# Two hybrid transformer blocks on one core: banks begun at their first product, four steps of side work later, filler products gone

## The reference, cut to what matters

```
first block, a layer:
  h = rms_norm(x) @ w_in          # queries, keys, values, index heads, gates: 10,052 columns
  y_a = attention over the 64 tokens that an indexer picks (top_k)  @ w_oa
  y_b = silu(layer_norm(conv31(glu)))  @ w_ob
  y_c = (gb * conv3(gc * xc))          @ w_oc
  y_d = stick-breaking attention       @ w_od
  x = x + (sum of sigmoid(gate_i) * y_i) @ w_merge
  x = x + (silu(conv3(h2 @ w_gate)) * (h2 @ w_up)) @ w_down
second block, a layer:
  c_q, c_kv, ... = split(rmsnorm(x) @ w_in_2)
  y_mla  = causal attention on up-projected latents (mla_mixer)
  y_gdn  = gated delta rule: gc = cumsum(g); decay = exp(gc_i - gc_j); triangular solve
  y_moba = block attention with a bias table
  x = x + concat(y_mla, y_gdn, y_moba) @ w_out
```

## Time and profile before

| | us |
|---|---|
| median of three runs | 1325.55 |
| lowest and highest run | 1325.3, 1328.61 |
| the profiled execution | 1327.21 |
| its span | 1325.4 |
| PE busy in it | 1301.4 (98%) |
| DVE, ACT busy | 1026.0 (77%), 746.5 (56%) |
| granted clock of PE, mean | 0.997 |

### The profile page before, as it was taken

How to read it: one execution, slowest core, us unless ns; L and a number is a source line. 1 busy time by engine, 2 the same in 40 slices (tenths; PEclk the granted TensorE clock), 3 DMA queues, 4 the chain that set the end, 5 groups by cost and what they waited for, 6 DMA issues and landing times. The chain is left out here.

```text
span 1325.4 us, 26400 instructions
## 1 busy us (share of the span) xinstructions
PE 1301.4 (98%) x10796; PEld 1240.3 (94%) x10796; DVE 1026.0 (77%) x1763; ACT 746.5 (56%) x1149; POOL 47.3 (4%) x48
## 2 busy tenths in 40 slices
PE   9999999999999999999999999999999999999997
PEld 8899999999999999999999989999989899888996
DVE  6899998677777677999997768777778746677565
ACT  6544566556454465544757556544567445586364
POOL 0000000000000000100000000000001100001100
PEclk9999999999999999999999999999999999999999
DMA  8565455565555465646365555665654223343232
GB/s 279 190 201 181 160 161 189 163 220 186 196 191 191 153 229 176 215 162 197 126 210 167 197 184 178 207 203 193 206 163 152 64 97 128 122 143 112 81 101 75
DMA packets 108991, 223.62 MB, mean 169 GB/s; under 512 B 6180, under 2 KB 17700, under 8 KB 108872
## 3 DMA queue, kind: packets, MB, share of 16 engines
q1 hardware_dynamic: 106736, 218.99, 49.5%
q10 hardware_dynamic: 2136, 2.96, 0.7%
HBM read 220.88 MB, written 1.06 MB: 167 GB/s over the span
## 5 line engine op out<-in xcount | busy, mean ns | idle before, releaser
L1191 ACT ACTIVATE whi<-ring 128x1024 fp32r<-128x1024 f32 (+3 forms) x430 | 433.7, 1027 | 343.2 <-PE bank L513 221.3
L1764 DVE TENSOR_TENSOR wlo<-ring,whi 128x1024 fp32r<-128x1024 f32 (+3 forms) x430 | 496.9, 1180 | 166.0 <-ACT whi L1191 133.1
L513 PE MATMUL bank<-hhi,whi 128*128 128x256 f32 x2016 | 272.5, 277 | 2.5 <-ACT hhi L1228 1.8
L522 PE MATMUL bank<-hhi,wlo 128*128 128x256 f32 x2016 | 273.0, 277 | 1.0 <-DVE wlo L1764 1.0
L513 PE MATMUL bank<-hlo,whi 128*128 128x256 f32 x2016 | 269.1, 276 | 0.0
L513 PEld LDWEIGHTS bank<-hhi,whi 128*128 128x128 f32 x2016 | 248.3, 192 | 5.5 <-issue 3.9
L522 PEld LDWEIGHTS bank<-hhi,wlo 128*128 128x128 f32 x2016 | 246.9, 192 | 4.9 <-issue 3.2
L513 PEld LDWEIGHTS bank<-hlo,whi 128*128 128x128 f32 x2016 | 247.3, 193 | 0.0
L1932 DVE SCALAR_TENSOR_TENSOR w<-w,par 128x256 f32<-128x256 f32 x240 | 98.1, 479 | 0.0
L535 PE MATMUL bank<-whi,hhi 128*128 128x512 f32 (+2 forms) x256 | 93.1, 366 | 0.0
L535 PE MATMUL bank<-whi,hlo 128*128 128x512 f32 (+2 forms) x256 | 92.6, 364 | 0.0
(11 more groups left out here) (311 smaller groups left out, 1549.1 us busy)
## 6 DMA issues: line engine op xcount, KB each, us to landing
ring<-in_w_in SPq DMA_DIRECT2D x100, 1024.0 KB, 5.1
ring<-in_w_ffn_down SPq DMA_DIRECT2D x22, 1024.0 KB, 5.1
ring<-in_w_ffn_gate SPq DMA_DIRECT2D x20, 1024.0 KB, 5.1
ring<-in_w_ffn_up SPq DMA_DIRECT2D x20, 1024.0 KB, 5.2
ring<-in_w_merge SPq DMA_DIRECT2D x8, 1024.0 KB, 5.2
ring<-in_w_out SPq DMA_DIRECT2D x8, 1024.0 KB, 5.0
ring<-in_w_oc SPq DMA_DIRECT2D x4, 1024.0 KB, 5.3
ring<-in_w_od SPq DMA_DIRECT2D x4, 1024.0 KB, 5.2
```

Source lines behind the costliest of these rows:

```text
L513: done = e.matmul(o, wh[:, k, cols(u)], paired(s_[:, k0 + k, :]), stop=False, skip_group_check=True, start=opens and k == 0 and s_ is sh a ...
L522: done = e.matmul(o, wl[:, k, cols(u)], paired(sh[:, k0 + k, :]), start=False, stop=closes, skip_group_check=True)
L1191: e.activation(part_of(whi, j), part_raw(j), ACT.Copy).then_inc(*up("hi.a"))
L1764: e.tensor_tensor(part_of(wlo, j), part_raw(j), part_of(whi, j), ALU.subtract).then_inc(*up("lo.v"))
```

## The change

It has five parts.

1. The "m" banks are taken when their first product is issued, not when the group begins (`Held`). The order of products and the numbers of the banks stay as they were; the wait for the second (and third) bank now stands before that bank's first product.
2. Two rounds of the search for the first half of the tokens move from place 67 to 70, and the last step of the search from 107 to 108.
3. The sum over tokens and the turning of the sums (`decay`) move from places 11 and 12 to 12 and 13.
4. The turned latent heads and the first logits (`latent`) move from 36 and 37 to 37 and 38.
5. The six unread products ahead of the sum go.

```diff
-        "indexer": [28, 51, 67, 67, 67, 67, 67, 67, 80, 80, 80, 80, 80, 88, 104, 105, 105, 105, 105, 107],
+        "indexer": [28, 51, 67, 67, 67, 67, 70, 70, 80, 80, 80, 80, 80, 88, 104, 105, 105, 105, 105, 108],
-        "decay": [10, 10, 11, 12],
+        "decay": [10, 10, 12, 13],
-        "latent": [26, 29, 30, 34, 36, 37, 39, 43, 46, 53, 54, 65, 66],
+        "latent": [26, 29, 30, 34, 37, 38, 39, 43, 46, 53, 54, 65, 66],
...
+        class Held:
+            def __init__(self, *begins):
+                self.begins, self.begun = begins, {}
+            def __getitem__(self, i):
+                if i not in self.begun:
+                    self.begun[i] = self.begins[i]()
+                return self.begun[i]
...
                 for name, kind, n, _ in MIX_IN:
-                    held = [ps.take(e, "m", name, l, i) for i in range(2)]
+                    held = Held(*(lambda i=i: ps.take(e, "m", name, l, i) for i in range(2)))
...
                 bk = ps.take(e, "s", "gsum", l)
-                awake(bk, 6)
                 e.wait_ge(*at("gv", l))
...
-                        heldv = [ps.take(e, "m", "cv", l, i) for i in range(2)]
-                        heldg = ps.take(e, "m", "cg", l)
+                        heldv = Held(*(lambda i=i: ps.take(e, "m", "cv", l, i) for i in range(2)))
+                        heldg = Held(lambda: ps.take(e, "m", "cg", l))
```

More of the change, by code:

```diff
@@ L769, in mix_p @@
                     for hf in range(2):
-                        held = [ps.take(e, "m", name, "gate", l, hf, i) for i in range(2)]
+                        held = Held(*(lambda i=i: ps.take(e, "m", name, "gate", l, hf, i) for i in range(2)))
                         for i in range(4):
@@ L775, in mix_p @@
                         put("second.p", name, "gate", l, hf)
-                        held = [ps.take(e, "m", name, l, hf, i) for i in range(2)]
+                        held = Held(*(lambda i=i: ps.take(e, "m", name, l, hf, i) for i in range(2)))
                         e.wait_ge(*at(key, l))
@@ L808, in ffn_p @@
                     for name in ("gate", "up"):
-                        held = [ps.take(e, "m", name, l, i6, i) for i in range((n + 1) // 2)]
+                        held = Held(*(lambda i=i: ps.take(e, "m", name, l, i6, i) for i in range(2)))
                         for i in range(4):
@@ L1124, in two_p @@
                     else:
-                        held = [ps.take(e, "m", name, l, i) for i in range(1 if name == "mg" else 2)]
+                        held = Held(*(lambda i=i: ps.take(e, "m", name, l, i) for i in range(2)))
                         for i in range(4):
@@ L1129, in two_p @@
                             else:
-                                chans(j, held, 2 * len(held), hh, 2 * i, i == 0, i == 3, between(j),
+                                chans(j, held, 2 if name == "mg" else 4, hh, 2 * i, i == 0, i == 3, between(j),
                                       ("two", l) if name == "kc" else None)
@@ L1161, in values_and_gate @@
                                 else:
-                                    done = e.matmul(hg[:, (u - 2) * S:(u - 2) * S + S], w_[:, k, cols(u)], paired(s_[:, k0 + k, :]),
+                                    done = e.matmul(hg[0][:, (u - 2) * S:(u - 2) * S + S], w_[:, k, cols(u)], paired(s_[:, k0 + k, :]),
                                                     start=begins, stop=closes and half_ == 1, skip_group_check=True)
```

## The result

The changed kernel takes 1333.21 us (median of four runs, 1332.39 to 1333.56) where the kernel before takes 1326.33 in the same comparison: a ratio of 1.0049, with a 95% interval of 1.0031 to 1.0066. That is 4 to 9 us more; 6.0 were forecast. The profiled executions differ by less, 1332.39 against 1327.21, since that of before was longer than its median and that of after the shortest of its four runs.

The account below looks back on a forecast made before the run. PE, busy 1301.4 of 1325.4 us, was taken to set the time, with DVE and ACT lacking slack where it waits. -1.2 + 3.2 + 1.5 + 0.8 + 1.7 = +6.0 on 1327.21, less 1.66: 1331.5 us; range 1320 to 1336.

Parts of the forecast that it names:

- the chain on DVE and ACT: Behind the moved sums: reading after taps, table load, weight halves, masks, copies; sum to squares takes 16.28 us.
- First block: Late banks and moved search rounds: PE's wait for L2178 goes, -0.6 us a layer, -1.2 in all.
- the cap: First block: PE can come at most 0.75 us earlier at 186.06, where it uses DVE's low half.
- Decay: Moved sum and turned sums, filler gone: squares start later, +3.2 us in the first layer, +1.5 in the second.
- the rival of a switch that costs more than the row shows: A table switch on ACT's chain takes twice the row's 1.28 us: +2.6, 1334.1 us; chance 0.03.
- The wait at the squares: First layer, squares' sums: PE arrives at 1008.2 and waits another 2.5 us for ACT.
- Latent heads and gate: Moved latent heads: L2335's wait goes, new bank wait about 1.0, gate 0.4 better; +0.4 us a layer, +0.8.
- Clock: PE's new idle stretches bring one uncovered fall to half clock: +1.7 us.
- gains that cancel the losses: Chain binds in the first layer alone (+3.2), other gains (-3.4) come in full: 1325.4 us; chance 0.27.
- every wait gained: Every wait that goes is gained, as DVE and ACT catch up: 12.9 us less, 1312.7; chance 0.08.
- a reading of the sums that doesn't bind: Reading not late enough to bind at the squares; parts 3 and 5 give -4.0: 1320.4 us; chance 0.10.
- the case of more falls: The clock falls in all four idle stretches, +6.8 us in place of 1.7: 1336.6 us; chance 0.05.

Follow-up runs that it names:

- b1_filler_at_gap: The changed kernel with nine unread products at the turned sums, where PE waits for DVE L2302: 1333.92 us, ratio 1.0061.
- a1_block1_held: The changed kernel with decay, latent heads and filler as before; only the late banks and the search's move are left: 1325.55 us, ratio 0.9995.
- e2_latent_alone: The kernel before with only the turned latent heads and first logits moved to places 37 and 38: 1328.09 us, ratio 1.0011.
- e1_decay_alone: The kernel before with only the sum and turned sums moved to places 12 and 13, the filler kept: 1333.78 us, ratio 1.0056.
- a4_sums_read_first: The changed kernel with decay listed ahead of the taps, so that DVE reads the sums first: 1333.4 us, ratio 1.0052.
- a3_latent_back: The changed kernel with the turned latent heads back at places 36 and 37: 1332.96 us, ratio 1.0049.
- a2_decay_back: The changed kernel with the sum and turned sums back at places 11 and 12, still no filler: 1331.08 us, ratio 1.0031.
- c1_before_no_filler: The kernel before without the six unread products, nothing else: 1329.32 us, ratio 1.0027.
- b2_filler_both: The changed kernel with nine unread products at the turned sums and nine more ahead of the squares' sums: 1332.17 us, ratio 1.0051.

## Why the prediction was right

The forecast was 1331.5, 6.0 us more; the medians differ by 6.9 and the two profiled executions by 5.2. Its mechanism held: the chain on DVE and ACT, and not PE, sets the start of the squares. That the sum fits so well is in part luck, since terms of it came out otherwise. By its terms, against the 5.2:

- **First block, -1.2: -0.8.** The wait for L2178 went, and the cap was met: PE's low products wait 0.33 for `wlo` L1775 at 179.61, ahead of the ones at 186.06 by which the sum was made. In the first layer PE was 1.3 us ahead at 113, where the wait of 1.0 for `wlo` went, and gave 1.0 of it back from 153 on, where the product of the third branch (`y_c @ w_oc`) waits 0.81 for DVE's `flo` L2125. That wait was not foreseen. It has the foreseen reason: the slower engines did not come sooner with PE; DVE starts this `flo` at 152.46, 0.29 earlier than before.
- **Decay, +3.2 and +1.5: +2.8 and +1.2.** From the sums to the squares the forecast had 16.28 us and the trace has 15.91 and 15.92, against 13.09 and, with half clock in it, 14.73 before. No link was missed; several were a little too long, since neighbours overlap (from 1004.89 to the copies at 1006.47 are 1.58 us, where two high halves were counted with 1.67). The stall at L2302 was put at 2.5 and is 2.29. The table load is followed by the exp 0.01 us later (998.09 + 1.28), and it stands 0.02 us behind the silu that ends at 998.07, not behind idle time, so the rival of a switch that costs more than the row shows falls. The Trainium skill, "ScalarE: Activation LUTs", section "What ACT_TABLE_LOAD costs", has the load as long as this trace (1.28 us); the drain that it adds, some 1.4 us more, does not show here. The sum itself started 0.63 earlier than before, where the forecast had it unmoved: DVE's gates came that much sooner, with the first block's gain.
- **The wait at the squares, 2.5 forecast: 0.58.** PE came 1.7 us later because the half clock fell into the stretch in which it would have waited. `b1_filler_at_gap`, without that fall, has 2.3.
- **Latent heads and gate, +0.4 a layer: +0.5.** The sum is right and parts of it are not. The gate's wait fell by 0.8 and PE passed that place 0.5 sooner (0.4 forecast): from the 64x64 products ahead of it to its low products are 4.73 us, 5.23 before. The new wait of the turned heads was put at 1.0 and is 0.65, and the solve's level lost 1.1 (0.4 forecast). The last follows from the gate's gain, as DVE and not PE says when the level can start; `a1_block1_held` shows both with the heads unmoved. `e2_latent_alone` gives the moved heads 1.5 us in all.
- **No term: -0.4 a layer.** From the first group of squares to the second PE took 13.76 us before, with a wait of 0.24 for L1592 at its end, and now 15.04, of which 1.7 are lost to the clock: 13.3 without. The wait is gone, and the group comes 0.4 sooner. Without this the terms add up to 5.9, with it to 5.1.
- **Clock, +1.7: +1.7 net, by another sum.** One uncovered stretch more was forecast. Its 1.7 us doesn't come out of the 4.0 us that the forecast names as its source; the two windows of before show it. There are two stretches more, one in each layer. In the first layer the stretch at 1023 went to 1012, and the new one at 998 was covered by the chain; in the second, that at 1170 became one at 1176, covered too, and the one at 1189 is new and uncovered. So the amount is right and the count of the forecast is not what gave it; that is luck.

Of the rivals, gains that cancel the losses are refuted by `e1_decay_alone`, every wait gained by `a1_block1_held`, and a reading of the sums that doesn't bind by the 2.27 us that PE waits at the squares in `b1_filler_at_gap`. The filler's loss was taken for a part of the case of more falls. Alone it costs 3.6 us, and together with the moved decay next to nothing (1333.21 without, 1333.78 for the moved decay with it). It did not keep the clock up there: `e1_decay_alone` has four stretches at half clock with the filler, as the changed kernel has without it. So each of the two, the moved decay with the filler kept and the missing filler with the decay in place, is enough for a loss. The effects don't add up, 7.9 for the decay alone, 3.6 for the filler, 2.2 for the latent heads by the medians, and 6.9 together.

## What to carry to other kernels

When an engine at 98% waits for one at 77%, follow the slower chain from the moved step to the next place where the busy engine needs its result; the wait that shows in the list (2.3 us at L2302) can be removed or filled without moving the end, as two experiments did. Moving a step by one place among other steps changes what stands ahead of it on each engine, and one set of taps or one half of the weights in between can cost up to its length: taking the reading out from behind 2.46 us of taps gave the chain back 1.3 (`a4_sums_read_first`). A filler that runs while the engine would wait anyway cost next to nothing here, and held the clock in one place and not in another; judge it by several runs' mean clock and times, since one profile can miss it.

## What the runs showed of the hardware

Each stretch at half clock between 12 and 1320 us lost the same 1.7 us in all thirteen kernels, wherever it came and however long the idle time ahead of it was (0.17 to 3.24 us). Two came in a row with 2.2 to 3.2 us of idle time at the squares of the first layer (`a3_latent_back`, `e1_decay_alone`, `b1_filler_at_gap`, `a4_sums_read_first`) and with 2.7 us at the sum (second layer of `a2_decay_back`), but only one with 2.27 us at the squares of the second layer of `b1_filler_at_gap`. The same idle time of 2.2 us at the sum was followed by a stretch in `a2_decay_back` and by none in the profiled execution of `c1_before_no_filler`, and 2.29 at the turned sums by one at 998 in the changed kernel and by none there in `a3_latent_back`.

Little idle time was not enough to keep the clock. Nine of the stretches (both in `b2_filler_both`; the one at 1023 in the kernel before, and six like it in four other runs) began 2.0 to 3.1 us after the start of a group of squares' sums, 16 products of one column in 1.9 us, with 0.17 to 0.24 us of idle time ahead of it. In the kernel before it is this group:

```profile
1021.22 1.92 PE L483 MATMUL bank<-onesb,w 128*128 128x1 f32 x16 [0.24 <-ACT w L1592]
```

`a1_block1_held` has the same group, at 1020.53 with 0.21 us of idle time, and no stretch behind it. What brings a fall is not settled by these runs.

On ACT, an ACTIVATE started 0.01 to 0.02 us behind its table load wherever its data were there (999.38 after 998.09 + 1.28).
